# The first pair's rows in the experts' loop: one fetch for four tiles, a one-hot product for the fifth, and 4 MB of weights released at another point

## What is computed

```python
h = rmsnorm(x, g_ffn)                                   # x is (544, 1024)
gi = argmax(h @ w_group + b_group)                      # one of 4 groups
el = (h @ w_router + b_router)[group gi]                # 8 experts of the group
pv, pi = top_k(softmax(el), 2)                          # two experts for a token
rows = zeros.at[dest].set(h[tok_sorted])                # tokens gathered by expert
out = (silu(xb @ w_gate[e]) * (xb @ w_up[e])) @ w_down[e]   # each expert, float32
y = segment_sum(out[dest] * weight, token)
```

## Time and profile before

| | us |
|---|---|
| median of 3 executions | 1032.11 |
| lowest, highest | 1029.98, 1034.71 |
| the profiled execution, its own time | 1029.85 |
| span of that execution in the trace | 1027.90 |
| mean granted clock of PE | 0.974 of full |

### The profile page before, as it was taken

One profiled execution on the slowest core, in us unless ns is written; L12 is line 12 of the kernel. 1 busy time (PEld: TensorE's weight loads), 2 busy tenths in 40 slices (PEclk: granted clock), 3 DMA queues, 4 the chain that ended last, 5 costly groups with the idle time before them and its releaser, 6 DMA issues.

```text
span 1027.9 us, 14164 instructions
## 1 busy us (share of the span) xinstructions
PE 921.3 (90%) x5699; PEld 585.5 (57%) x5702; DVE 375.8 (37%) x967; ACT 255.9 (25%) x523; POOL 134.4 (13%) x143
## 2 busy tenths in 40 slices
PE   7989999989999999998999888887887888888996
PEld 6859995456999998983333322222322222234775
DVE  4179997854323445352111110101101001112796
ACT  6154327765222232231000000000000000001542
POOL 2304442213110000001111111011010011000000
PEclk9999999999999999998999998999999989999998
DMA  9860602004643406377999999999999999996601
GB/s 265 111 163 2 205 2 62 2 1 126 209 122 104 120 4 267 109 276 279 428 422 429 427 428 426 425 427 425 428 426 428 425 426 427 428 423 244 255 21 67
DMA packets 60132, 263.72 MB, mean 257 GB/s; under 512 B 11054, under 2 KB 36030, under 8 KB 46224
## 3 DMA queue, kind: packets, MB, share of 16 engines
q1 hardware_dynamic: 54160, 250.99, 63.6%
q0 software_dynamic: 5296, 9.79, 2.6%
q10 hardware_dynamic: 624, 2.23, 0.6%
HBM read 253.99 MB, written 16.85 MB: 263 GB/s over the span
## 4 chain that ended last, share of the span: by engine, by line
PE 62%; DMA 30%; DVE 4%; ACT 2%; issue 1%; SPq 1%; DVEq 0%; ACTq 0%
DMA arena<-in_w_up 26%; PE ps L1135 13%; PE ps L1302 12%; PE ps L992 5%; PE ps L1167 4%; PE ps L1450 4%; PE ps L1327 3%; PE ps L892 3%; PE ps L963 3%; DMA arena<-in_w_ple 2%; PE ps L1061 2%; PE ps L1082 2%; PE ps L1031 2%; PE ps L1423 1%; PE ps L899 1%
## 5 line engine op out<-in xcount | busy, mean ns | idle before, releaser
L1302 PE MATMUL ps<-arena,hT 128*64 128x512 f32 x960 | 238.7, 651 | 35.8 <-DMA arena<-in_w_up 35.5
L1302 PEld LDWEIGHTS ps<-arena,hT 128*64 128x64 f32 x960 | 71.9, 143 | 199.5 <-issue 151.2
L2236 DVE TENSOR_TENSOR xf<-xf,ps 128x256 f32<-128x256 f32 x32 | 13.5, 421 | 402.1 <-ACT xf L1731 379.5
L1135 PE MATMUL ps<-arena_merge,arena_merge 128*128 128x256 f32 x624 | 99.7, 287 | 0.0
L1327 PE MATMUL ps<-arena,xf 128*64 128x512 f32 x336 | 76.7, 598 | 12.8 <-DVE xf L2239 12.8
L847 POOL DMA_INDIRECT expert_rows<-xf,arena x32 | 32.1, 1002 | 426.1 <-ACT xf L1735 400.2
L1135 PEld LDWEIGHTS ps<-arena_merge,arena_merge 128*128 128x128 f32 x624 | 87.5, 188 | 0.0
L1135 PE MATMUL ps<-xf_merge,arena_merge 128*128 128x256 f32 x480 | 82.0, 288 | 0.0
L1731 ACT ACTIVATE xf<-ps 128x256 f32<-128x256 f32 x30 | 11.5, 384 | 259.4 <-PE ps L1302 259.4
L1135 PEld LDWEIGHTS ps<-xf_merge,arena_merge 128*128 128x128 f32 x480 | 69.3, 188 | 0.0
L1735 ACT ACTIVATE xf<-ps 128x512 f32<-128x512 f32 x30 | 17.9, 597 | 159.8 <-PE ps L1327 159.8
(11 more groups left out here) (309 smaller groups left out, 1290.7 us busy)
## 6 DMA issues: line engine op xcount, KB each, us to landing
arena<-in_w_gate SPq DMA_DIRECT2D x30, 2048.0 KB, 28.8
arena<-in_w_up SPq DMA_DIRECT2D x30, 2048.0 KB, 36.8
arena<-in_w_down SPq DMA_DIRECT2D x11, 2048.0 KB, 36.6
hT<-in_w_down SPq DMA_DIRECT2D x11, 2048.0 KB, 35.6
arena<-in_w_down SPq DMA_DIRECT2D x20, 1024.0 KB, 30.4
arena<-in_w_in SPq DMA_DIRECT2D x10, 1024.0 KB, 6.3
arena<-in_w_in SPq DMA_DIRECT2D x3, 2048.0 KB, 11.5
arena<-in_w_gate SPq DMA_DIRECT2D x8, 512.0 KB, 8.8
```

What stands on the lines that cost most here:

```text
L1135: mm = pe.matmul(w[:, 2 * lo_t:lo_t + hi_t], rounded(st[:, c, cols]), rounded(mv[:, c, lo_t:hi_t]), start=c == 0 and k == 0, stop=c == pla ...
L1302: mm = pe.matmul(ps[g * BLK:(g + 1) * BLK, 2 + s, :], xsT[:, c, col:col + BLK], expert_columns(k, slice(0, 2), c, g), start=c == 0, stop=c ...
```

## The change

The last tile's index product goes to columns of its own (32 to 63 of bank 7), so the table of the first four steps is complete after `index(3)`. DVE makes the first pair's `gather_of` column from it ahead of `choose(4)`, and keeps a copy for the sum with the last tile's part later. POOL clears `xs[0]`, behind its unchanged wait for `xn_stored` 64, and issues the first fetch when `index_ready` is 1; the second and third follow at `index_ready` 2. The last tile's rows for that pair are not fetched: DVE makes a one-hot of place, scaled by the row's reciprocal norm (`last_tile_hot`), and PE multiplies `x_nat` of tile 3 by it into banks 0 and 1 (`last_tile_rows`, 8 products). The fetched rows are then turned by 8 products with the identity that add to the same banks (`early_tiles_rows`), in place of the 8 turns. The `keep_busy` products become one, ahead of `ranks(4)`. SP's wait on `xs_in[0]` is gone, the one on `rows_full` 5 stays.

```diff
@@ SP
         sp.wait_ge(rows_full, TILES)
-        sp.wait_ge(xs_in[0], 16)
         load_planes(2, 1, 5, 8)
@@ POOL
         pool.wait_ge(xn_stored, 16 * 4)
+        link(pool.memset(xs[0], 0.0))
+        pool.wait_ge(index_ready, 1)
+        gather(xs[0], gather_of[:, 0:1], xs_in[0])
         pool.wait_ge(sample_stored, 16)
-        pool.wait_ge(index_ready, 1)
-        for p in range(3):
+        pool.wait_ge(index_ready, 2)
+        for p in range(1, 3):
             gather(xs[p], gather_of[:, p:p + 1], xs_in[p])
-        pool.wait_ge(index_ready, 2)
+        pool.wait_ge(index_ready, 3)
@@ PE
+        def last_tile_rows():
+
+            w = wide(0).rearrange("p (c t) -> p c t", c=KD)
+            for c in range(KD):
+                pe.matmul(w[:, c, :], x_nat[:, 3, c:D:KD], first_hot.rearrange("p s n -> p (s n)"),
+                          start=c % (KD // 2) == 0, stop=False)
+
+        def early_tiles_rows(half):
+
+            w = wide(0).rearrange("p (c t) -> p c t", c=KD)
+            for c in range(half * KD // 2, (half + 1) * KD // 2):
+                mm = pe.matmul(w[:, c, :], xs[0][:, c:D:KD], ident[:, :], start=False, stop=c % (KD // 2) == KD // 2 - 1)
+            return mm
...
         logits(4)
+        keep_busy(1)
         ranks(4)
+        pe.wait_ge(place_ready, TILES)
+        last_tile_rows()
         index(4)
...
-        pe.wait_ge(turn_out, TILES)
-        keep_busy(3)
-        pe.wait_ge(index_ready, 3)
+        pe.wait_ge(xs_in[0], 16)
+        early_tiles_rows(0).then_inc(turn_full, 1)
+        early_tiles_rows(1).then_inc(xsT_full, 1)
+        pe.wait_ge(index_ready, 4)
...
-        pe.wait_ge(xs_in[0], 16)
-        rows_turned(0, 0, KD // 2).then_inc(turn_full, 1)
-        rows_turned(0, KD // 2, KD).then_inc(xsT_full, 1)
-        keep_busy(1)
@@ DVE
+        def last_tile_hot():
+
+            i, t = TILES - 1, ROUTE[TILES - 1]
+            link(dve.tensor_scalar(rt_pen[:, 0:2], picks[:, t, 0:2], nrm[:, 5 + t:6 + t], None, ALU.mult))
+            dve.wait_ge(ranks_full, i + 1)
+            rank = ps[:, RANKS_BANK[i], RANKS + EXPERTS * i:RANKS + EXPERTS * i + 2]
+            link(dve.tensor_tensor(first_hot, rt_place.unsqueeze(1).to_broadcast([P, 2, BLK]),
+                                   rank.unsqueeze(2).to_broadcast([P, 2, BLK]), ALU.is_equal))
+            dve.tensor_tensor(first_hot, first_hot, rt_pen[:, 0:2].unsqueeze(2).to_broadcast([P, 2, BLK]), ALU.mult)\
+                .then_inc(place_ready, 1)
...
         rows_rstd_of(4)
+        dve.wait_ge(index_done, TILES - 1)
+        rows_to_gather(ps[0:BLK, 7, 0:2], 0, 1)
+        link(dve.tensor_copy(rt_cnt[0:BLK], ps[0:BLK, 7, 0:EXPERTS]))
         choose(4)
+        last_tile_hot()
         place(4)
-
         dve.wait_ge(index_done, TILES)
-        w = ps[0:BLK, 7, 0:EXPERTS]
...
+        w = rt_t1[0:BLK, 0:EXPERTS]
+        link(dve.tensor_tensor(w, rt_cnt[0:BLK], ps[0:BLK, 7, EXPERTS:2 * EXPERTS], ALU.add))
+        rows_to_gather(w[:, 2:], 1, PAIRS)
```

More of the change, by code:

```diff
@@ L402, in _program @@
     rt_over = rt(work, [1])
+    first_hot = place_hot[:, 1]
     picks = at(69.25, [TILES, EXPERTS], BF16)
@@ L1212, in index, with keep_busy @@
             t, r = ROUTE[i], ROWS[ROUTE[i]]
-            pe.wait_ge(place_ready, i + 1)
+            pe.wait_ge(place_ready, i + 1 + i // (TILES - 1))
             for k in range(2):
-                mm = pe.matmul(ps[0:BLK, 7, 0:EXPERTS], place_hot[0:r, i % 2, k, :], pick[0:r, t, k, :],
-                               start=i == 0 and k == 0, stop=i == TILES - 1 and k == 1)
+                mm = pe.matmul(ps[0:BLK, 7, i // (TILES - 1) * EXPERTS:(1 + i // (TILES - 1)) * EXPERTS], place_hot[0:r, i % 2, k, :], pick[0:r, t, k, :],
+                               start=i in (0, TILES - 1) and k == 0, stop=i >= TILES - 2 and k == 1)
             mm.then_inc(index_done, 1)
+        def keep_busy(n):
+            for _ in range(n):
+                pe.matmul(ps[:, 2, :], ident[:, :], g_fin[:, 0:512], start=True, stop=True)
+        def last_tile_rows():
[8 more added lines that the diff above has]
+            return mm
         pe.wait_ge(late_out['act'], LATE[('gb', 6)].out)
@@ L1276, in _ @@
         mm.then_inc(index_done, 1)
-        pe.wait_ge(turn_out, TILES)
-        def keep_busy(n):
-            for _ in range(n):
-                pe.matmul(ps[:, 2, :], ident[:, :], g_fin[:, 0:512], start=True, stop=True)
-        keep_busy(3)
-        pe.wait_ge(index_ready, 3)
+        pe.wait_ge(xs_in[0], 16)
+        early_tiles_rows(0).then_inc(turn_full, 1)
+        early_tiles_rows(1).then_inc(xsT_full, 1)
+        pe.wait_ge(index_ready, 4)
         def rows_turned(k, lo=0, hi=KD):
@@ L2189, in place, with rows_to_gather @@
             ins.then_inc(place_ready, 1)
+        def rows_to_gather(marks, lo, hi):
+            link(dve.tensor_scalar(rt_ti[0:BLK, 2 * lo:2 * hi], marks, -1.0, None, ALU.add))
+            for h in range(2):
+                ins = dve.tensor_scalar(gather_of[h * BLK:(h + 1) * BLK, lo:hi].bitcast(I32), rt_ti[0:BLK, 2 * lo + h:2 * hi:2],
+                                        1, None, ALU.arith_shift_right)
+            ins.then_inc(index_ready, 1)
+        def last_tile_hot():
[7 more added lines that the diff above has]
+                .then_inc(place_ready, 1)
         add_rows(0, 0)
@@ L2259, in pair @@
                 turned_rows(xsT, w, P).then_inc(xsT_ready, 1)
-        dve.wait_ge(index_ready, 3)
+        dve.wait_ge(index_ready, 4)
         link(dve.tensor_tensor(rt_cmp, rt_cnt.unsqueeze(2).to_broadcast([P, EXPERTS, PER]),
```

5 lines of the change are left out of this document (removed).

## The result

| | before | after |
|---|---|---|
| median of 7 executions each, us | 1031.12 | 1038.17 |
| lowest, highest | 1029.74, 1034.71 | 1036.92, 1041.60 |
| ratio, 95% interval | | 1.0065 [1.0044, 1.0085] |
| profiled execution: time, span | 1029.85, 1027.90 | 1040.63, 1038.80 |
| mean granted clock of PE | 0.974 | 0.966 |

The change costs 6.7 us (4.5 to 8.8), 0.65% of the time, with an interval that begins at 0.44%. That is inside the stated range, but twice the forecast (+3.4) and near to rival 2 (+7.1).

The account below looks back on a forecast made before the run. The continuous DMA weight queue was taken to bound the expert stage. Store, clearing, fetch and turn put first gate and up at 478.1; less 474.7 gives +3.4 us, so 1035.5 us from median 1032.11; range 1029.8 to 1039.5.

Parts of the forecast that it names:

- rival 2: Last store and first fetch queue behind the released 4 MB, slower than forecast: shift +7.1 us, 1039.2 us; chance 0.18.
- a landing later than 474.8: First fetch's rows landing after 474.8 us in the trace's clock, named as the sign of rival 2; forecast landing 472.9.
- the formula: Shift of the expert stage's end = start of first gate and up + 7.6 + 1.8 - 484.1 us.
- clearing and start of the fetch: On POOL between store and fetch: clearing xs[0] about 0.95 us plus waits, 0.5 to start; fetch at 467.6.
- The store: Last tile's store amid released weights: 0.8 us added, landing 466.0, bounds 465.2 and 466.4.
- The fetch: First fetch amid the 4 KB held pieces: 5.3 us against 4.3 alone, landing 472.9, bounds 470.9 and 476.7.
- The turn: Fetched rows' turn on PE, now 16 passes at half clock: about 4.1 us instead of 1.14; 2.3 at full clock.
- rival 1: PE's clock holds at the turn, store and fetch hardly slowed: shift -0.2 us, 1031.9 us; chance 0.23.
- The last tile's product at no cost: PE's new product, 2.3 to 4.5 us, through by 468 to 470, covered by the fetch's landing at 472.9.
- Rival 3: First fetch goes early, at 461.2, without waiting for the last store: shift -3.4 us, 1028.7 us; chance 0.05.
- the yardstick: DMA byte count from 468 on, giving expert 3's effective start before, 484.1, and shift = first gate-and-up start less 474.7 us.

Follow-up runs that it names:

- e9: Kernel before with keep_busy(15) in place of keep_busy(3) ahead of the first pair's turn, delaying PE only; ratio 1.0064, +6.6 us.
- e2: Kernel before with only SP's wait for the first fetch removed, so the held 4 MB go out early; ratio 1.0038, +3.9 us.
- e1: Kernel after with SP's wait for the first fetch put back ahead of the held 4 MB; ratio 1.0002, +0.2 us.
- e5: Kernel after, but the first fetch doesn't wait for the last tile's store, whose rows are filled early with tile 0's; ratio 0.9998, -0.2 us.
- e4: Kernel after, but SP releases the held 4 MB only once the last tile's store has landed; ratio 1.0058, +6.0 us.
- e6: Kernel after with 10 keep_busy products in place of 1, meant to keep PE's clock up; ratio 1.0076, +7.8 us.
- e11: Kernel before with unused products and turns added on PE, stationary columns 8 apart or adjacent; its one execution took 1037.37 us.
- e7: Kernel of e5 with SP's wait for the first fetch back, so the 4 MB are held; ratio 1.0018, +1.9 us.
- e8: e7 with the fetched rows' products first on PE, count and later index behind, DVE's scaling earlier, keep_busy products added; ratio 0.9989, -1.1 us.
- e10: e8 with normed rows regrouped by ACT so stationary operands have adjacent columns, the last tile's product taking those rows; ratio 0.9974, -2.7 us.
- e12: Kernel before with the first pair's 8 turns replaced by 8 products with the identity; ratio 1.0019, +2.0 us.

## Why the prediction came out as it did

Most of the forecast's path held, and by its own sign, a landing later than 474.8, rival 2 is what happened. The fetch still waited for the last store, the released 4 MB left a hole behind them instead of ahead, gate and up with its issue took 7.6 us (492.41 - 484.80), and the delay went to the end: the formula gives +7.1 for the trace, and e9 shows it by a delay of PE alone. That the result lies in the range comes from the range's upper end, which took in most of rival 2; 0.77 stood on a difference of less than 0.5%, and 0.65% was measured. Two terms of the sum carry the miss.

| from the store's issue | forecast | measured |
|---|---|---|
| store landed | 5.0 | 8.1 |
| clearing and start of the fetch | 1.6 | 1.2 |
| fetch, to the turn | 5.4 | 6.5 |
| turn, then to gate and up | 5.1 | 5.0 |
| sum | 17.1 | 20.8 |

- **The store** is the step that failed: I took 5.0 us and bounded it by 5.4, by letting every packet of the store wait for one packet of weights. It took 8.1, in e2 7.9, against 3.9 in e1, where the weights are held and all else is equal. The 4.1 us between them are 27 packets of 4 KB at 426/16 GB/s, for 8 packets of the store on an engine: over three packets of weights for each. By the rule named under rival 2 (the Trainium skill, DMA: Bandwidth & Descriptors, section on queues, rings and completion order) an engine drains several descriptors before it switches; that more than one packet went ahead of each agrees with it, but no run here separates that rule from another that gives unequal turns.
- **The fetch** was scaled down by the size of the pieces, to 5.3 us. It took 6.5, 7.8 in e2, 8.7 in e5 and 9.0 in e4, against 3.6 to 5.3 with the weights held. Scaling by the size of the packets beside it was wrong: next to pieces of 4 KB it lost 2.2 to 4.7 us against the 4.3 of before, where 1.0 had been allowed from a scatter's 3.5 next to 16 KB. The traces suggest that it goes with how much is still queued when the fetch starts, though no run tests that alone: 9.0 where the 4 MB were still being issued (e4), 8.7 where the last of them had been issued 1 us before (e5), 7.8 and 6.5 where that was 9 to 10 us before (e2 and after).
- **The turn** came out at the forecast 4.1 us, for a wrong reason. I put it down to half clock, which the trace of after indeed shows (0.50 from 476.8 to 483.3). e6 has it at 4.18 and the product at 4.09 with the clock high, and e11 shows the stride of the stationary operand as the cause. At full clock I would have said 2.3; rival 1 rested on that figure, and with 4.1 in its place its sum gives +1.6 and not -0.2.
- **The last tile's product at no cost** held in the kernel after: it ends at 472.75, and the rows land at 479.8. It held only because the store and the fetch were slow. In e1, e5 and e7 PE is last, and 2.1 us of each group are the stride's. I had named 3 us as the point from which it would be the bound, with 2.3 us for the group and not 4.1.

Rival 2 named the mechanism that decided, the sharing of the DMA engines. Its total agrees to 0.1 us (its own terms add up to 481.9, for which 481.8 was written), but that is in part luck, for its split does not: 5.4 for the store and 8.3 for the fetch, where 8.1 and 6.5 were measured. Its chance of 0.18 was too low. Rows of both kinds spoke for it (12.5 us for a fetch amid loads), and I set them aside for a scaling that no row had shown. Rival 3, the early fetch, did not come true, and e5 shows what it was worth: even with the store out of its way the kernel only draws level, since the fetch meets the released weights and PE is last with two groups of 4.1 us.

So the gain meant by the change was lost twice. The release delays the fetch on which everything waits, and it can bring nothing in return, since expert 3's load waits for the first gate and up. The early index brings nothing while the fetch waits for the store. With both undone and PE's order changed (e8) no gain can be told from none; with the stride removed too (e10) the idea is worth 2.7 us (0.8 to 4.5).

What stays open: e2 measured +3.9 where its trace gives +5.9; the trace is of one execution, and the interval ends at 5.6. Why e7 scatters is not known. e10 changed order, clock and stride against the kernel after together; e8 to e10 isolates the layout of the rows, and there the traces show the products in half the time, but the intervals of the two runs overlap, and no run has the adjacent columns without the reordering. The first fetch moved 0.27 MB in the change and its variants and 0.34 in the kernel before, which has the last tile's rows in it; its times in the two are compared above as if they were the same. In the yardstick the three fetches of before were put at 0.84 MB, and the trace has 0.94, which would lower every worked-out shift by 0.2 us.

## What to carry to other kernels

Before moving a bulk load to an earlier point, find the small transfer that the critical path waits for in that time. If the load's bytes aren't what is late, holding them until the small transfer has landed costs nothing, and releasing them cost 4 to 7 us here. Where a turn is replaced by a float32 product, look at the stride of the stationary operand: here it doubled the time at full clock, half clock added next to nothing to that, and it stayed hidden as long as something else was later.

## What the hardware showed that I had not expected

- A 512 KB store in 4 KB rows landed in 3.1 to 4.6 us with the weights held (3.1 in e4 and e12, 4.6 in e10) and in 7.9 to 8.5 with 4 MB of weights in 4 KB pieces beside it (after, e2, e5 and e6). An indirect fetch of 0.27 or 0.34 MB took 3.6 to 5.3 with the weights held (e1, e10) and 6.5 to 9.0 beside them (after, e4).
- A float32 load of 128 columns as stationary operand took 193 ns with adjacent columns and 332 ns with columns 8 elements apart in products, 141 and 192 in turns.
- The granted clock fell behind idle times of PE as short as 2.13 us (e6, at 484.9, in the middle of the turn that followed, which had PE busy for 2.9 us) and 2.94 us (e4), and it came back only in the middle of the gate and up that followed, which then took 9.59 and 9.29 us instead of 7.4.
